# First request group of a streaming encoder layer: constants and first weights loaded in another order, the sample scores issued one unit ahead, cache keys and cache values loaded by separate steps

## The reference, cut to what matters

```python
mod = silu(c) @ w_ada + b_ada              # c: 17 vectors of 1024; w_ada: 1024 x 6144
h = LN(x) * (1 + scale1) + shift1
q, k, v = columns of h @ w_in              # 16 heads of 64, here as 8 pairs of heads

z = einsum(q, k) * HD ** -0.5              # prompt: keys of the prompt; samples: 1024 cached keys + 16 new
mask = k_pos < q_pos
log_rest = where(mask, log_sigmoid(-z), 0)
after = cumsum(log_rest, reverse) - log_rest
a = where(mask, exp(log_sigmoid(z) + after), 0)
o = a @ v
```

## Time and profile before

| what | value |
|---|---|
| median of 3 runs | 4868.33 us (4856.72 to 4876.36) |
| profiled execution, its time | 4863.06 us |
| its span in the trace | 4861.2 us |
| TensorE busy over the span | 3451.5 us (71%) |
| VectorE, ScalarE, GpSimd busy | 2755.5, 930.4, 2549.8 us |
| mean granted TensorE clock | 0.807 of full speed |
| `norm` of group 0 | 0 to 49.4 us |
| `stick` of group 0 | 49.4 to 497.05 us |

### The profile page before, as it was taken

The page is one execution under the profiler, slowest core; times in us unless marked ns, Lnnn a source line. Parts: engine busy times, 40 slices in busy tenths (PEclk is TensorE's granted clock), DMA queues, the critical chain, the costliest instruction groups (busy, mean ns, idle before and its releaser), DMA issues.

```text
span 4861.2 us, 46453 instructions
## 1 busy us (share of the span) xinstructions
PE 3451.5 (71%) x16090; PEld 1711.0 (35%) x16090; DVE 2755.5 (57%) x6532; ACT 930.4 (19%) x2008; POOL 2549.8 (52%) x2359
## 2 busy tenths in 40 slices
PE   5787989887888879877899887799763333333355
PEld 3354665454544534333444345444320000000000
DVE  2233331358986765567777766644787666664420
ACT  2244230013442210011444422200110000000000
POOL 0000000005466666656677665656577777777775
PEclk8798999988999989988999998899875555555565
DMA  5766223339899999999999998989999999999997
GB/s 226 292 233 232 95 85 124 117 143 333 283 333 333 362 374 393 416 351 400 347 405 394 326 357 329 362 346 417 354 357 389 404 394 383 397 392 400 419 401 307
DMA packets 445319, 1580.58 MB, mean 325 GB/s; under 512 B 48328, under 2 KB 87624, under 8 KB 434720
## 3 DMA queue, kind: packets, MB, share of 16 engines
q0 software_dynamic: 338080, 1231.18, 65.9%
q1 hardware_dynamic: 105104, 344.78, 19.2%
q10 hardware_dynamic: 1904, 1.65, 0.1%
HBM read 1527.99 MB, written 49.43 MB: 324 GB/s over the span
## 4 chain that ended last, share of the span: by engine, by line
PE 41%; POOL 17%; DMA 16%; DVE 12%; issue 9%; ACT 4%; ACTq 0%; SPq 0%; DVEq 0%; POOLq 0%
DMA peer_v_ring<-in_peer_v,expertsT 11%; POOL peer_v_ring L2326 9%; POOL peer_u_ring L2318 8%; PE bank L2386 6%; PE wide L1356 5%; PE wide L1775 4%; PE wide L2057 4%; PE bank L713 3%; DVE peer_u_ring L2477 3%; PE wide L1344 3%; PE bank L1775 2%; PE wide L778 2%; PE bank L723 1%; PE wide L788 1%; DMA mod_w<-in_w_ada 1%
## 5 line engine op out<-in xcount | busy, mean ns | idle before, releaser
L2318 POOL DMA_INDIRECT peer_u_ring<-in_peer_u,experts x1152 | 1287.3, 1117 | 820.9 <-DVE peer_u_ring L2477 409.1
L2477 DVE SCALAR_TENSOR_TENSOR peer_u_ring<-peer_u_ring,peer_h 128x1024 f32<-128x1024 f32 x1152 | 1385.4, 1221 | 526.3 <-DMA peer_u_ring<-in_peer_u,experts 482.9
L2386 PE MATMUL bank<-peer_v_ring,peer_lone 128*32 128x512 f32 x4608 | 853.9, 823 | 941.0 <-DMA peer_v_ring<-in_peer_v,expertsT 825.1
L2326 POOL DMA_INDIRECT peer_v_ring<-in_peer_v,expertsT x1152 | 1232.9, 1070 | 477.5 <-issue 296.7
L2386 PEld LDWEIGHTS bank<-peer_v_ring,peer_lone 128*32 128x32 f32 x4608 | 115.4, 124 | 1527.1 <-issue 1479.7
L2287 POOL MEMSET peer_lone<- 128x1087 f32 x1 | 1.0, 1003 | 984.3 <-SPq L269 984.3
L1356 PE MATMUL wide<-w_ring,hT 128*128 128x256 f32 x1152 | 278.3, 401 | 32.8 <-DVE gla_v L1694 32.8
L713 PE MATMUL bank<-hT,w_ring 128*128 128x384 f32 x768 | 264.9, 494 | 18.2 <-DMA w_ring<-in_weights 15.9
L2057 PE MATMUL wide<-mT,w_ring 128*128 128x384 f32 x768 | 269.6, 501 | 10.4 <-DMA w_ring<-in_weights 7.4
L1356 PEld LDWEIGHTS wide<-w_ring,hT 128*128 128x128 f32 x1152 | 228.6, 202 | 100.9 <-issue 67.8
L1121 DVE SCALAR_TENSOR_TENSOR sb_l<-sb_z,sb_l 128x768 f32<-128x768 f32 (+2 forms) x120 | 95.5, 796 | 169.4 <-ACT sb_l L996 169.1
(11 more groups left out here) (281 smaller groups left out, 4544.5 us busy)
## 6 DMA issues: line engine op xcount, KB each, us to landing
w_ring<-in_weights SPq DMA_DIRECT2D x312, 512.0 KB, 6.6
sb_kc<-in_kcT SPq DMA_DIRECT2D x16, 2048.0 KB, 11.6
sb_vc<-in_vc SPq DMA_DIRECT2D x16, 2048.0 KB, 7.3
mod_w<-in_w_ada SPq DMA_DIRECT2D x24, 1024.0 KB, 5.9
peer_u_ring<-in_peer_u,experts POOLq DMA_INDIRECT x1152, 6.5
peer_v_ring<-in_peer_v,expertsT POOLq DMA_INDIRECT x1152, 6.4
scores<-sel_sc SPq DMA_DIRECT2D x6, 1024.0 KB, 8.9
peer_sc_half<-scores POOLq DMA_DIRECT2D x12, 512.0 KB, 7.6
```

Of the source, the lines that this page charges most:

```text
L2318: pool.indirect_dma_start(self.u_ring[:, n % NU, :], None, K.A["peer_u"], bass.IndirectOffsetOnAxis(ap=K.ids_of[:, j % CHOSEN, k:k + 1], a ...
L2326: pool.indirect_dma_start(self.v_ring[:, m % NV, :], None, K.A["peer_v"], bass.IndirectOffsetOnAxis(ap=K.ids_of_turned[:, j % CHOSEN, t:t ...
L2386: last = pe.matmul(self.F.psum[strip:strip + 32, :], self.lone[:, mark - at:mark - at + 32], self.v_ring[:, m % NV, c * HALF:(c + 1) * HAL ...
L2477: dve.scalar_tensor_tensor(u, u, 1.0, self.h2[:, j % 2, :], ALU.mult, ALU.mult, accum_out=self.dots[:, j % 2, k:k + 1]).then_inc(self.dot_ ...
```

## The change

Only the start and `stick` of group 0 have another order; other groups keep theirs. No computation is added or dropped.

```diff
@@ start @@
-MARGIN, AHEAD, CONSTS = 14, 6, 12
+MARGIN, AHEAD, CONSTS = 14, 6, 11
...
                 act.dma_start(mods.c[:, :], A["cT"]).then_inc(mods.c_in, 16)
-                act.dma_start(K.ident[:, :], A["ident"]).then_inc(K.const_in, 16)
+                act.dma_start(K.ident[:, :], A["ident"]).then_inc(mods.bias_in, 16)
                 act.dma_start(mods.bias[:, :, :], A["b_ada"]).then_inc(mods.bias_in, 16)
+                act.wait_ge(mods.c_in, 16)
+                act.activation(mods.silu[:, :], mods.c[:, :], ACT.Silu).then_inc(mods.silu_done, 1)
...
-                mods.load(sp, 0, K.banks[6])
+                mods.load(sp, 0, K.banks[6], 0, 3)
+                norm.load(sp, GROUPS[0])
+                mods.load(sp, 0, K.banks[6], 3, KC)
+                K.feed(sp, GROUPS[0], STICK_AT)
@@ Stick.sync @@
+        def keys(u):
...
+            if u < 2 * SB_PAIRS:
+                sp.dma_start(self.kc[:, :, :], A["kcT"][p][:, 4 * half:4 * half + 4, :]).then_inc(self.kc_in, 16)
+        def values(u):
...
             if u:
                 sp.wait_ge(K.banks[7].full, K.banks[7].full_at["co", u - 1])
...
-                caches(2 * p + 1)
+                keys(2 * p + 1)
+                values(2 * p + 1)
+                if p:
+                    keep_output(p - 1)
                 if 1 <= p <= 2:
                     self.mods.store(sp, p, self.P1)
                 if p < 2:
                     self.mods.load(sp, p + 1, self.P1)
                 if p + 1 < SB_PAIRS:
-                    caches(2 * p + 2)
+                    keys(2 * p + 2)
             K.feed(sp, G, STICK_AT + 3 * min(p + 2, SB_PAIRS))
             if p + 1 < SB_PAIRS:
                 keep(p + 1)
-            keep_output(p)
+            if G.sample:
+                if p + 1 < SB_PAIRS:
+                    values(2 * p + 2)
+            else:
+                keep_output(p)
@@ tensor_early @@
+        self.c_scores(pe, G, 0)
         for p in range(SB_PAIRS):
...
-            i, u = 2 * p, 2 * p
-            self.c_scores(pe, G, u)
+            i, u, second = G.hi * p, 2 * p, G.hi > 1
             self.scores(pe, G, i)
+            next(ahead, None)
+            next(ahead, None)
             if p:
                 self.c_out_turn(pe, G, u - 1)
+            self.c_scores(pe, G, u + 1)
+            self.to_here(pe, G, i)
             next(ahead, None)
             next(ahead, None)
-            self.to_here(pe, G, i)
-            next(ahead, None)
+            self.c_turn(pe, G, u)
             self.later_keys(pe, G, i)
...
             for _ in ahead:
                 pass
+            self.c_out_turn(pe, G, u)
+            if second:
+                self.later_keys(pe, G, i + 1)
+            self.c_turn(pe, G, u + 1)
+            if p + 1 < SB_PAIRS:
+                self.c_scores(pe, G, u + 2)
+            if second:
+                self.values(pe, G, i + 1)
             self.c_values(pe, G, u + 1)
@@ scalar_early @@
...
+            if more:
+                self.keep_q(act, G, p + 1)
             if p:
                 self.c_keep_out(act, G, u - 1)
-            if more:
-                self.keep_q(act, G, p + 1)
+            self.c_weights(act, u)
+            self.c_take(act, G, u + 1)
+            self.c_take_log(act, u + 1)
             self.weights(act, G, i)
```

More of the change, by code:

```diff
@@ L341, in __init__, with load @@
         self.slots = [k % len(self.w) for k in range(KC)] + [k % self.FEW for k in range((self.ROUNDS - 1) * KC)]
-    def load(self, sp, r, bank):
-        for n in range(r * KC, (r + 1) * KC):
+    def load(self, sp, r, bank, lo=0, hi=KC):
+        for n in range(r * KC + lo, r * KC + hi):
             slot = self.slots[n]
@@ L378, in dve @@
             dve.wait_ge(self.K.const_set, 1)
-            dve.wait_ge(self.bias_in, 16)
+            dve.wait_ge(self.bias_in, 32)
         acc = bank.filled(dve, ("mod", r))
@@ L421, in sync, with load @@
         K.start(sp, G, "norm")
+        if G.n:
+            self.load(sp, G)
+        K.end(sp)
+    def load(self, sp, G):
         for i, t in enumerate(G.tiles):
-            sp.dma_start(self.x[:, i, :], rows(K.A["x"])[t]).then_inc(self.x_in[i], 16)
-        K.end(sp)
+            sp.dma_start(self.x[:, i, :], rows(self.K.A["x"])[t]).then_inc(self.x_in[i], 16)
     def steps_before(self, G):
@@ L677, in sync @@
         if G.sample:
-            caches(0)
+            keys(0)
+            values(0)
         K.feed(sp, G, STICK_AT + 3)
@@ L894, in tensor_early @@
             ahead = self.project(pe, G, p + 1) if p + 1 < SB_PAIRS else iter(())
[L895 to L896 removed]
+            i, u, second = G.hi * p, 2 * p, G.hi > 1
             self.scores(pe, G, i)
+            next(ahead, None)
+            next(ahead, None)
             if p:
                 self.c_out_turn(pe, G, u - 1)
+            self.c_scores(pe, G, u + 1)
+            self.to_here(pe, G, i)
             next(ahead, None)
             next(ahead, None)
[L902 to L903 removed]
+            self.c_turn(pe, G, u)
             self.later_keys(pe, G, i)
[L905 removed]
+            if second:
+                self.scores(pe, G, i + 1)
             next(ahead, None)
             self.values(pe, G, i)
[L908 to L909 removed]
+            self.c_values(pe, G, u)
+            if second:
+                self.to_here(pe, G, i + 1)
             next(ahead, None)
[L911 to L916, removed]
[L917 to L919 removed]
             if p < 2:
@@ L2561, in _ @@
                     for stage in stages:
+                        if G.n == 0 and stage is stick:
+                            act.wait_ge(K.const_set, 4)
                         stage.scalar(act, G, beside)
-                        if G.n == 0 and stage is norm:
-                            act.wait_ge(K.const_in, 16 * CONSTS)
                 beside.to_end()
```

75 lines of the change are left out of this document (38 added, 37 removed).

## The result

| | before | after |
|---|---|---|
| median, same chip (4 runs each) | 4862.83 us | 4938.46 us (4924.9 to 4943.62) |
| ratio after / before | | 1.0147 (95% interval 1.0116 to 1.0179) |
| profiled execution, its time | 4863.06 us | 4940.8 us |
| its span | 4861.2 us | 4938.9 us |
| first `c_scores` | 83.00 | 67.33 |

The change costs 75.6 us (by the interval 56 to 87), where the sum forecast +36.1; 4904 us was forecast, with a range to 4934. The time is 34 us beyond the forecast and the change 39.5, since the median before came out at 4862.83 with a fourth run, 5.5 under the 4868.33 that the forecast stood on. Ahead of `gla` the kernel is 65.5 us late; the other 10 to 12 us come behind it.

What follows compares the result with a forecast made beforehand. It took group 0 as a serial head, with TensorE close to the bound in its pairs. Terms -18.9 + 10.2 + 13.2 + 35.5 - 3.9 = +36.1 on 4863.1 gave 4899.2, plus 5.3 to the median: 4904 us, range 4852 to 4934.

Steps and rivals of the forecast that it cites:

- the three waits: TensorE's waits in a later pair: first keys 3.3 us, VectorE's turned copy 2.7, second turn 2 then keys 1.7.
- start, first `c_scores`: Kernel start: earlier x, weights and constants bring the first `c_scores` from 83.0 to 64.1, -18.9 us.
- five later pairs: Pairs 2 to 6 of `stick`: 51.5 us each against 44.4, +7.1 each, +35.5 in all.
- last pair to `gla`: Last pair of `stick` to its end: 46.4 us against 50.3, -3.9.
- The clock: Later pairs: TensorE's lower clock behind waits costs 1.7 us in the first half and 1.5 in the second, 3.2 together.
- sum at the full clock: A later pair laid out step by step with TensorE at full clock: 48.3 us against 44.4.
- half two: A later pair from the end of `c_values(u)`, at 30.5 us, to the pair's end at 48.3, at full clock.
- Pairs 0 and 1: First two pairs, with transfer-bound `Mods` rounds and 14.6 us behind each: 80.9 and 84.2 us, +10.2 and +13.2.
- Nearly one to one: Group 0 is a serial head; what `stick` gains or loses is shifted through to the kernel's end.
- Much slower: the half clock stays: Rival: TensorE at half clock through the later pairs, period 57 us, 4931 us and more; chance 0.10.
- No change: keys in time: Rival: keys land by 9 us after issue in later pairs, period 44 us, total 4860 us; chance 0.20.
- Faster: Rival: TensorE never waits in the pairs, -45 us over five, total 4817 us; chance 0.12.

Runs made afterwards that it cites:

- e11: The changed kernel unaltered, profiled again on another chip; 4943.57 us, ratio 1.0148 to the kernel before.
- e4: Changed kernel with VectorE's copies of a turned bank ahead of the next unit's sums, keys still late; ratio 1.0049 to the kernel before.
- e10: Changed kernel with VectorE's copies ahead of its sums and extra small products while TensorE waits for keys; ratio 1.0039 to the kernel before.
- e1: Kernel before with only the change's new start, `stick` in its old order; 4996.92 us, ratio 0.9989 to the kernel before.
- e2: Changed kernel with the old start, so the new `stick` order alone; 5089.65 us, ratio 1.0171 to the kernel before.
- e5: Changed kernel with both keys issued ahead of values and VectorE's copies ahead of sums; ratio 0.9926 to the kernel before.
- e6: e5 with the rounds of `Mods` moved to the end of pairs 0 and 1; ratio 0.9894 to the kernel before.
- e9: e6 with turned output, `kn` and second turn ahead of `new`, and ScalarE's weights and output copies earlier; ratio 0.9831 to the kernel before.
- e3: Changed kernel with SP issuing each load of keys ahead of the values it stood behind; ratio 1.0028 to the kernel before.
- e8: Changed kernel with extra small products, adding no result, while TensorE waits for keys; 5068.83 us, ratio 1.0125 to the kernel before.

## Why the prediction was wrong in size

The direction and the three waits were right; what they cost TensorE through its clock was not, nor when the keys land, and the time was 34 us beyond. By the prediction's own terms, each with the mark that measures it:

| term | forecast | measured | off by |
|---|---|---|---|
| start, first `c_scores` | -18.9 | -15.7 | +3.2 |
| pair 0 | 80.9 | 86.3 | +5.4 |
| pair 1 | 84.2 | 88.8 | +4.6 |
| five later pairs | 257.5 | 272.7 | +15.2 |
| last pair to `gla` | 46.4 | 47.4 | +1.0 |
| head in all | +36.1 | +65.5 | +29.4 |

**The term that failed is "The clock": 3.2 us a pair.** The five later pairs cut at the prediction's own marks, means in us, with its sum at the full clock (48.3) beside them:

| stretch of a pair | sum | changed | e11 | e4 | e10 |
|---|---|---|---|---|---|
| start to first keys | 12.3 | 12.8 | 12.8 | 12.8 | 12.8 |
| their products | 1.9 | 3.6 | 3.5 | 3.6 | 2.3 |
| to the third turned bank | 9.5 | 9.4 | 9.4 | 7.6 | 7.3 |
| to the end of `c_values(u)` | 6.8 | 8.3 | 9.5 | 6.8 | 6.8 |
| to the second keys | 13.2 | 13.7 | 13.5 | 13.5 | 13.3 |
| to the pair's end | 4.6 | 6.7 | 6.7 | 6.7 | 6.0 |
| pair | 48.3 | 54.5 | 55.4 | 50.9 | 48.5 |

The first key products cost 1.7 more than at full clock, which I had priced. The stretch behind the third bank costs 1.5 more in the mean (2.7 in e11), priced at nothing: I put the low clock behind the key wait and behind half two, and forgot it behind the 2.7 us wait for VectorE that I had worked out myself. With that wait cut to 0.35 (e4, e10) the stretch takes the 6.8 of the list. Behind the second keys 2.1 were lost where I took 1.5. So the clock costs some 5.3 us a pair and not 3.2. The other 1.0 us is the keys: they come 0.5 later in each half, for I had taken the least of the earlier trace rows (11.8), not its median (12.5). Over five pairs that is about 10 us by the clock and 5 by the landing, the 15.2 of the table. The sum at the full clock is thus near right.

In the pair of the rows above, the longest, the clock costs 1.7 + 3.0 + 2.7 = 7.4 us: 9.8 us pass from the third bank (323.36) to the end of `c_values(u)` (333.14), and 7.3 from the second keys (345.89) to the pair's end. In the last two of the five the stretch behind VectorE's wait takes 6.8, at full clock, behind a wait of 1.8 us; in the other three that wait was 2.0, 2.6 and 2.8 us, and the clock fell. Why it falls in one pair and not in the next is not shown.

**Pairs 0 and 1** erred for the same reason at two places. What follows a round took 17.4 us in pair 0 (136.2 to 153.6), not 14.6, its tile of v and key products running at the half clock (3.78 and 3.34 us). The other 4.4 us of pair 0 lie ahead of the round: 34.3 us from the first `c_scores` (67.33) to the load of values at 101.60, not 29.9. There the same two stretches ran at the half clock: the key products took 3.80, and from the third bank to the end of `c_values(0)` 9.8 us passed, not 6.8:

```profile
78.50 3.80 PE L836 MATMUL wide<-sb_kc,sb_qd 128*32 128x512 f32 x16 [1.71 <-DMA sb_kc<-in_kcT]
...
91.74 0.33 PE L845 MATMUL wide<-ident,sb_cz 128*128 128x128 f32 x1 [2.76 <-DVE sb_caT L1172]
...
95.17 3.73 PE L739 MATMUL bank<-w_ring,hT 128*128 128x128 f32 x16
```

In e4, without that wait, the end of `c_values(0)` comes 5.4 us earlier. The round itself took 1.8 less than taken.

**The start** was 3.2 short of the gain, 2.2 of it by the last `w_ada` load. That an earlier `c_scores` is not all kept is shown by e1: 15.8 us earlier there, 11.9 at the stage's end. My sum passed the start on whole.

**"Nearly one to one" to the end** stands within what the runs can tell. GpSimd starts 64.0 us later than in the earlier trace rows, as `stick` ends 65.5 later:

```profile
L2312 POOL MEMSET peer_lone<- 128x1087 f32 x1 | 1.0, 1004 | 1048.3 <-SPq L269 1048.3
```

The 10.1 us that the medians have beyond the head's 65.5 are no proof of a loss behind it, since 65.5 lies inside the interval of the change (56 to 87 us). In the profiles the stretch from the first gather to the end takes 3781.4 us (e11: 3781.2) against 3767.8 before, and the extra comes behind the last group's stages, where only gathers are left. But e10, which ran in e11's job, shows 3766.8 in an execution 14.4 us under its own median, so this stretch may well move by as much from one execution to the next; that is not shown, and a small loss behind the head is not ruled out. The medians beyond the head differ by job and not by how late the head is: 5.0 us more in e11 and 3.6 in e10, only 2.3 in e2, whose head is the latest of all, and 6 to 9 us less in e4, e5, e6 and e9.

**The rivals.** "Much slower: the half clock stays" was nearest in time (4931 and more) and in part right: the low clock is not there throughout (0.79 to 0.81 over a pair) but in two or three stretches. It was near by luck: it came to 4931 by a period of 57, where 54.5 was measured and the other terms made up the rest. "No change: keys in time" is what e3 built (keys land after 7.4 us): 47.4 a pair, not 44, as it too had left out the clock behind the wait for sums. "Faster" needed both conditions that the prediction named for it, keys early and copies not behind sums: no gain beyond that of the start came before e5. There it passed 0.5% (32.6 us) with pairs of 42.7, not under 39.7, since the last pair took 33.9 us instead of 50.3 before. A period under 39.7 was reached in e9 alone.

## What to carry to other kernels

When an order written by hand gives an engine new short waits, price each twice: its length, and the TensorE work behind it at 1.2 GHz; here the second came to 5.3 us a pair in the mean, and to 7.4 in the longest, against waits there of 4.7, 2.6, 1.9 and 0.6. For a landing take the median of the rows and not the least. To bring a load forward it has to be moved past whatever its queue waits for, not only written as a step of its own: the keys, apart from the values but still behind them, landed no sooner, and one position further up gave back 7 us a pair. Look at what each engine does between a chain's end and its next use, since the gain of issuing one unit ahead appears only when no engine puts later work in front of it (42.7 us with two such places mended, 38.6 in the last kernel, from 54.5).

## What had not been expected of the hardware

Waits of 1.9 to 4.7 us, some 15 us apart, were enough to bring TensorE to the 1.2 GHz level two or three times a pair; where no wait was over 1 us (the two windows of e9) it kept 1.00. Products without use in a wait brought the key products behind it to full clock in three pairs of five (L840 in 1.92 us, not 3.64) and shortened the stage by 15.4 us in e10 beyond e4, but by little in e8, where another wait followed. And the chips of different jobs gave the same kernel 4863, 4871, 4991 and 5007 us, nearly all of it, by the profiles of the other kernels, behind the first gather; a head of 12 us gained (e1) is hardly seen in a total.
